# Conditioning products of the second network moved along VectorE's queue, and all their weight loads issued by GpSimd

## The reference, cut to what matters

```python
# first network, layer l
mod = (silu(c) @ w_ada[l] + b_ada[l]).reshape(b, 6, d)
sh_a, sc_a, gt_a, sh_f, sc_f, gt_f = [mod[:, i, None, :] for i in range(6)]
u = rms_norm(x, g_mix[l]) * (1 + sc_a) + sh_a          # ... three attention branches
x = x + gt_a * (merged @ w_out[l])
u = rms_norm(x, g_ffn[l]) * (1 + sc_f) + sh_f
x = x + gt_f * ((silu(u @ w_ffn_gate[l]) * (u @ w_ffn_up[l])) @ w_ffn_down[l])

# second network, layer i: the same with two vectors, for the tokens and for a context of 256 more
mod_lat = silu(c_2) @ ada_w_2[i] + ada_b_2[i]          # sh1, sc1, g1, sh2, sc2, g2
mod_ctx = silu(c_ctx_2) @ ada_w_2[i] + ada_b_2[i]
h = rmsnorm(x) * norm_g[i, 0] * (1 + sc1) + sh1        # i = 0: neighbourhood attention and spatial gating
x = x + g1 * rmsnorm(mixer(h), norm_g[i, 1])           # i = 1: retention, whose output is for the tokens alone
h = rmsnorm(x) * norm_g[i, 2] * (1 + sc2) + sh2
x = x + g2 * rmsnorm((silu(gate) * up) @ w_out, norm_g[i, 3])   # gate, up = dwconv3(h @ w_in)
```

## Time and profile before

| | us |
|---|---|
| median of 3 runs | 2406.58 (2398.55 to 2410.11) |
| the profiled execution | 2400.64 |
| its span | 2398.5 |
| PE busy | 2195.0 (92%) |
| DVE busy | 1633.2 (68%) |
| ACT busy | 1179.0 (49%) |
| POOL busy | 32.3 (1%) |

### The profile page before, as it was taken

One profiled execution on the slowest core, in us unless ns is written; L12 is line 12 of the kernel. 1 busy time (PEld: TensorE's weight loads), 2 busy tenths in 40 slices (PEclk: granted clock), 3 DMA queues, 4 the chain that ended last, 5 costly groups with the idle time before them and its releaser, 6 DMA issues.

```text
span 2398.5 us, 36407 instructions
## 1 busy us (share of the span) xinstructions
PE 2195.0 (92%) x13724; PEld 1925.3 (80%) x13724; DVE 1633.2 (68%) x2618; ACT 1179.0 (49%) x2032; POOL 32.3 (1%) x18
## 2 busy tenths in 40 slices
PE   1899999999999999999787979799998999898998
PEld 0797888999997889999674658578776888888998
DVE  5558876983658876973777688938484823565983
ACT  3355574653555655654534534435253323645763
POOL 4000000000000000000000000000000000000000
PEclk8899999999999999999898999899999999999999
DMA  6357734865557625864352145435351423214553
GB/s 264 132 177 237 230 112 158 270 216 176 165 190 236 215 97 177 294 206 158 117 182 88 54 157 176 158 105 201 107 176 61 141 93 118 97 55 139 187 184 114
DMA packets 107181, 385.08 MB, mean 161 GB/s; under 512 B 11664, under 2 KB 16272, under 8 KB 105744
## 3 DMA queue, kind: packets, MB, share of 16 engines
q1 hardware_dynamic: 75680, 272.66, 34.1%
q10 hardware_dynamic: 31344, 110.24, 13.3%
HBM read 381.81 MB, written 1.05 MB: 160 GB/s over the span
## 4 chain that ended last, share of the span: by engine, by line
PE 74%; DVE 13%; DMA 5%; ACT 5%; issue 2%; ACTq 1%; DVEq 0%; SPq 0%
PE ps L882 19%; PE ps L885 18%; PE ps L886 18%; DVE ada_junk L1935 5%; DMA work<-adas_in 4%; PE ps L899 3%; PE ps L902 3%; PE ps L903 3%; DVE ring_l L1910 2%; PE ps L1294 1%; DMA ring<-tape_in 1%; PE ps L915 1%; PE ps L918 1%; PE ps L919 1%; PE ps L1159 1%
## 5 line engine op out<-in xcount | busy, mean ns | idle before, releaser
L882 PE MATMUL ps<-part,ring_l 128*128 128x256 f32 (+1 forms) x3640 | 1123.6, 309 | 42.4 <-DVE part L1910 32.3
L885 PE MATMUL ps<-part,ring_r 128*128 128x256 f32 (+1 forms) x3640 | 1112.1, 306 | 0.0
L886 PE MATMUL ps<-part,ring_r 128*128 128x256 f32 (+1 forms) x3640 | 1110.9, 305 | 0.0
L1910 DVE TENSOR_TENSOR ring_l<-ring,ring_r 128x1024 fp32r<-128x1024 f32 x511 | 616.5, 1221 | 307.5 <-ACT ring_r L1341 304.9
L882 PEld LDWEIGHTS ps<-part,ring_l 128*128 128x128 f32 x3640 | 691.7, 190 | 95.8 <-DVE part L1910 38.9
L1341 ACT ACTIVATE ring_r<-ring 128x1024 fp32r<-128x1024 f32 x511 | 531.2, 1054 | 397.7 <-DMA ring<-tape_in 264.1
L885 PEld LDWEIGHTS ps<-part,ring_r 128*128 128x128 f32 x3640 | 690.2, 190 | 32.0 <-issue 1.2
L886 PEld LDWEIGHTS ps<-part,ring_r 128*128 128x128 f32 x3640 | 690.1, 190 | 30.8
L1935 DVE SCALAR_TENSOR_TENSOR ada_junk<-work 128x1024 bf16<-128x1024 f32 x272 | 345.7, 1271 | 39.2 <-DMA work<-adas_in 23.1
L899 PE MATMUL ps<-ring_l,part 128*128 128x512 f32 x264 | 106.3, 403 | 12.4 <-ACT work L1747 6.4
L902 PE MATMUL ps<-ring_r,part 128*128 128x512 f32 x264 | 105.9, 401 | 0.0
(11 more groups left out here) (226 smaller groups left out, 2052.5 us busy)
## 6 DMA issues: line engine op xcount, KB each, us to landing
ring<-tape_in SPq DMA_DIRECT2D x518, 512.0 KB, 3.3
work<-adas_in ACTq DMA_DIRECT2D x176, 512.0 KB, 4.3
work<-ada_first_in ACTq DMA_DIRECT2D x8, 1024.0 KB, 16.2
work<-bias_in ACTq DMA_DIRECT2D x1, 2048.0 KB, 7.9
work<-cond_in ACTq DMA_DIRECT2D x1, 1536.0 KB, 8.0
x<-x_t_in ACTq DMA_DIRECT2D x1, 1024.0 KB, 12.8
x<-ctx_in ACTq DMA_DIRECT2D x1, 1024.0 KB, 8.5
x<-dist_in ACTq DMA_DIRECT2D x1, 1024.0 KB, 8.5
```

The source lines that it names most:

```text
L882: mm = pe.matmul(dst, lhsT=wl, rhs=mr, start=(k == 0), stop=False)
L885: pe.matmul(dst, lhsT=wr, rhs=mr, start=False, stop=False)
L886: mm = pe.matmul(dst, lhsT=wr, rhs=ml, start=False, stop=(k == len(moving) - 1))
L1910: return dve.tensor_tensor(dst, whole, rounded_part.bitcast(F32), ALU.subtract)
```

## The change

Two things change, and no product is added or dropped.

First, all 176 loads are issued from POOL's queue, in two loops written at its end. POOL waits once for the first group of the first layer (`fox_f`), then, tile by tile, for the same semaphore for which ACT waited. ACT's queue no longer holds loads or their waits.

Second, DVE's products in the second network stand elsewhere. The 12 beside `na_qk` stay; none stand after the mixing products; 12 tiles stand beside `out0_0`; the other 56 stand in the wide feed-forward: one beside each of `conv0_0` to `conv0_15`, two beside each of `conv0_16` to `conv0_21`, and now also beside the output tiles (one beside each of `out1_0_f`, two beside `out1_1_0` to `out1_1_3`, one beside each of the twelve others). `modulation2` and `gain2` are called in smaller portions, each before its first reader.

```diff
-        ADA2_PAIRS = (6, 9)
-        ADA2_BEFORE = N_ADA - 2 * FT
-        def ada2_beside(f):
-            return range(ADA_LATE + ADA2_BEFORE + 2 * f, ADA_LATE + ADA2_BEFORE + 2 * f + 2)
+        ADA2_PAIRS = 6
+        ADA2_NORM = 3 * KD
+        ADA2_BESIDE, ada2_next = {}, ADA2_NORM
+        for c, (per_conv, per_out) in enumerate(((1, (1,) * KD), (1, (2,) * 4 + (1,) * 4), (2, (1,) * KD))):
+            for f in made_before(0, c):
+                ADA2_BESIDE[f"conv{f}"] = range(ada2_next, ada2_next + per_conv)
+                ada2_next += per_conv
+            for f in range(KD):
+                ADA2_BESIDE[f"out{c}_{f}"] = range(ada2_next, ada2_next + per_out[f])
+                ada2_next += per_out[f]
...
@@ gpsimd, after the first seven panels
+            pool.wait_ge(*done("fox_f", 0))
+            for l in range(DEPTH):
+                for t in range(N_ADA):
+                    if t >= ADA_SLOTS:
+                        pool.wait_ge(*ada_made(ada_last(t - ADA_SLOTS), l))
+                    elif l > 0:
+                        pool.wait_ge(*ada_made(ada_last(N_ADA - ADA_SLOTS + t), l - 1))
+                    pool.dma_start(ada_slot(t), adas[l * N_ADA + t]).then_inc(ada_landed[t % ADA_SLOTS], 16)
+            for t in range(ADA_LATE + N_ADA):
+                if t >= ADA_SLOTS:
+                    pool.wait_ge(*ada2_made(ada2_last(t - ADA_SLOTS)))
+                else:
+                    pool.wait_ge(*ada_made(ada_last(N_ADA - ADA_SLOTS + t), DEPTH - 1))
+                pool.dma_start(ada_slot(t), adas[DEPTH * N_ADA + t]).then_inc(ada_landed[t % ADA_SLOTS], 16)
@@ scalar, first network (and the same for load_ada2 and load_ada2_pair in the second)
-                def load_ada(t):
-                    if t >= ADA_SLOTS:
-                        act.wait_ge(*ada_made(ada_last(t - ADA_SLOTS), l))
-                    act.dma_start(ada_slot(t), adas[l * N_ADA + t])\
-                        .then_inc(ada_landed[t % ADA_SLOTS], 16)
...
@@ vector, second network
             ahead2("na_v3")
-            ada2_pairs(*ADA2_PAIRS)
...
-            for n in range(ADA2_PAIRS[1], ADA_LATE // 2):
+            for n in range(ADA2_PAIRS, ADA2_NORM // 2):
...
-            dve.wait_ge(*ada2_made(ada2_last(ADA_LATE - 1)))
-            modulation2(0, ADA_EARLY, N_ADA, 3)
+            dve.wait_ge(*ada2_made(ada2_last(ADA2_NORM - 1)))
+            modulation2(0, ADA_EARLY, ADA_EARLY + ADA2_NORM, 3)
...
             norm_in(2, 2, 3)
-            ada2_pairs(ADA_LATE // 2, (ADA_LATE + ADA2_BEFORE) // 2)
-            def beside(f):
-                for t in ada2_beside(f):
+            def beside(place):
+                if place == "out1_0":
+                    dve.wait_ge(*ada2_made(ada2_last(ADA_LATE - 1)))
+                    modulation2(0, ADA_EARLY + ADA2_NORM, N_ADA, 8)
+                    gain2(0, 3, 10)
+                for t in ADA2_BESIDE[place]:
                     ada2(t)
             feed_forward2(0, beside)
+            dve.wait_ge(*ada2_made(ada2_last(ADA_LATE + N_ADA - 1)))
+            modulation2(1, 0, ADA_EARLY, 0)
+            gain2(1, 0, 2)
             norm_out(1, 3)
             dve.wait_ge(*y2_scaled(2 * KD - 1))
-            dve.wait_ge(*ada2_made(ada2_last(ADA_LATE + N_ADA - 1)))
-            modulation2(1, 0, N_ADA, 0)
-            for n in range(4):
-                gain2(1, n, 2 + 2 * n)
             norm_in(3, 0, 0)
+            modulation2(1, ADA_EARLY, N_ADA, 3)
+            for n in range(1, 4):
+                gain2(1, n, 3 + 2 * n)
```

More of the change, by code:

```diff
@@ L2356, in feed_forward2 @@
                     rests(last)
+                    if c == 0:
+                        for f in range(KD):
+                            ahead2(f"out{1 + 2 * j}_{c}_{f}")
+                            beside(f"out{c}_{f}")
                     if c > 0:
```

50 lines of the change are left out of this document (12 added, 38 removed).

## The result

| | before | changed |
|---|---|---|
| median | 2405.41 us (4 runs) | 2375.18 us (2372.26 to 2382.55, 4 runs) |
| ratio | | 0.9881, interval 0.9848 to 0.9914 |
| ratio in a second series (5 rounds) | | 0.9918, interval 0.9890 to 0.9945 |
| span of the profiled execution | 2398.5 us | 2369.9 us |
| PE busy, mean granted clock | 2195.0, 0.962 | 2182.2, 0.968 |

The change is worth 0.8 to 1.2%, 20 to 29 us, by the ratios of the two series; forecast were 14.6, and 2388 us in a range of 2368 to 2420. The span of the profiled execution fell by 28.6 us. The terms of the sum did not all come out, as the stages show.

The account below looks back on a forecast made before the run. PE was taken to bound the kernel, busy 92% of the span. Terms 17.7 + 1.8 + 3.7 - 2.65 - 6.0 = 14.6 us gained, from 2400.6 to 2386.0, or 2392.0 by the median; forecast 2388, range 2368 to 2420.

Parts of the forecast that it names:

- First part of the wide feed-forward: At the start of `out1_0`: 20 fewer DVE products ahead end most of PE's wait and its slower clock; gain 17.7 us.
- Before the neighbourhood attention: Six loads leave ACT, so it copies the values earlier; gain 1.8 us, most of PE's 13.06 us gap stays.
- `out0_0`: Gating layer's output projection: 12 tiles instead of 14 bring `norm_out` earlier; gain 6.8 - 5d, 3.7 us.
- d: Time by which a load issued by POOL lands later than one issued by ACT; taken as 0.62 us from the cast.
- Beside `na_qk`: Twelve tiles there: ACT's late issues give back 0.45 us, later landings cost 5d; -2.65 us.
- First network: Attention, 64 tiles: eight waits without slack and steps with little slack, all charged to the span; -6.0 us.
- (A): Rival: POOL's loads land no later, d between 0 and 0.3; 19 to 27 us gained, 2374 to 2382; chance 0.22.
- the sign that the prediction named: Median from issue to landing of an ada tile, 4.3 us before: 4.9 by forecast, 4.3 to 4.6 by (A), over 5.7 by (B).
- (B): Rival: landing time decides in the 32 attention steps, 42 us per us beyond 1.34 us slack; slower, 2415 at 1.73; chance 0.14.
- (C): Rival: POOL writing load descriptors and DVE hold each other up, 88 loads at 0.62 us, 55 us, 2441; chance 0.08.
- (D): Rival: PE's wait at `out1_0` stays, from hidden tiles' rests and splits; gain there 3 to 10, 2394 to 2401; chance 0.11.
- closing tests of the prediction: Wrong if landing grows over 1.3 us and time still falls, or landing unchanged within 0.2 brings under 15 us.

Follow-up runs that it names:

- the block back: Changed kernel with two tiles again beside each of conv0_1 to conv0_8 and none beside out1_0_f; ratio to before 0.9952.
- second profile: The changed kernel profiled again, nothing altered, in a second series; ratio to before 0.9918.
- five memsets: Changed kernel with five small waited-for POOL memsets between wait and issue of each load, their target behind all other tiles; ratio to before 0.9977.
- the shifted one with five: Changed kernel with five POOL memsets before each load's issue and their 32-byte target ahead of the work area, moving it; ratio to before 1.0031.
- the shift alone: Changed kernel with 32 unused bytes of SBUF ahead of the work area, nothing else changed; ratio to before 0.9937.
- two memsets: Changed kernel with two small waited-for POOL memsets between wait and issue of each load, their target behind all other tiles; ratio to before 0.9913.
- the same shift and two memsets: Changed kernel with two POOL memsets before each load's issue and their 32-byte target ahead of the work area; ratio to before 0.9994.

## Why the prediction held, and where it did not

By the steps of the prediction, with the cuts of the table (profile of before against that of the changed kernel):

- **First part of the wide feed-forward**: forecast 17.7, measured 127.7 - 110.2 = 17.5. The reasoning held in both halves: PE stands for 2.43 us where 3.12 had been taken over from the next joint, and its clock no longer falls (1.00 against 0.62). The kernel with the block back shows the cause, and the one with ACT's loads at the new places has the same 110.2.
- **Before the neighbourhood attention**: forecast 1.8, measured 106.3 - 101.9 = 4.4 (2.9 in the second profile); PE's idle time in the stage fell by 3.0 in both, from 17.8 to 14.8. Mis-sized, and for a wrong reason. I took PE's L1216 at 1280.45 for the end of the values; they had been ready for copying earlier, as the kernel with POOL loads and old places shows, where ACT copies at 1277.16. What then decides is DVE: it was busy with products up to 0.34 us before ACT's part was ready, so they had to go too, which the term left out.
- **`out0_0`**: forecast 3.7, measured 73.4 - 70.3 = 3.1 (1.8 in the second profile). That the first two agree is luck. The term was 6.8 - 5d, so with ACT's loads, d = 0, it would be 6.8; the kernel with ACT's loads at the new places has the same 70.3. What the term had wrong is how early ACT and PE allow `norm_out`. The prediction took 4.5 us from PE's L1159 at 1405.73 to the end of ACT's root; in the rows themselves the root ends at 1413.51 + 0.63 = 1414.14, 8.4 us behind it, because PE's 16 products of the sums of squares take 7.03 us. That leaves 1417.38 - 1414.14 = 3.2 us to be won. Now DVE waits for that root, 0.51 us in the changed kernel and 2.40 with ACT's loads. In the second profile of the changed kernel it does not wait, so with POOL's landings DVE and the root are about even there.
- **Beside `na_qk`**: forecast -2.65, measured -1.2. With ACT's loads the stage took 67.5 and 66.4 us, with POOL's and the same products in it, without delay or shift, 67.0 to 69.0; so about -1 can be said.
- **First network**: forecast -6.0, measured -0.2 (353.4 to 353.6). This is the step that failed. d was about right where DVE feels it: 0.65 by the free slot, against 0.62 chosen, though 0.26 of it is the way to the issue, which the cast from which 0.62 was taken does not hold; that the two agree is partly luck. DVE's waits grew, by 2.9 us in the two stretches. The failed step is "DVE and PE are nearly even here, so I charge the whole of it to the span". The runs show about 2 us of PE's idle time in its place (13.6 with ACT's landings, 15.6 with POOL's), and stretches of the attention that are not longer (353.9 us with ACT's loads and 353.1 with POOL's, in the mean). Only with later landings does the charge become what the formula says: at five memsets the attention is 12.4 us longer than in the changed kernel's profile; at two it is 3.3 longer, which undelayed kernels reach too (356.8). Which instruction of the step gives DVE this slack was not measured.
- **Not in the sum**: 4.1 us in the tail (526.4 to 522.3) and 1.1 in the rest of the wide feed-forward. The prediction has no term for the tail, and the change touches no instruction in it; PE's pace differed there. In the changed kernel two thirds of the products of 256 columns in the thin feed-forward followed each other at 113.3 ns, in its second profile nearly all, and before all at 117.8. So this seems to belong to the kernel and not to the execution, but what in the kernel sets it is open.

Together 17.5 + 4.4 + 3.1 - 1.2 - 0.2 + 4.1 + 1.1 = 28.8, of 28.6 measured in the spans. Without the tail's pace the change is worth some 24 us in this profile. The ratios hold the tail too and can't part the two.

Of the rivals, (A), d between 0 and 0.3, has the time that came out, 2374 to 2382, and by the sign that the prediction named it would be taken for true: from issue to landing the median is 4.6, within the 4.3 to 4.6 of (A) and below the 4.9 of the forecast. But that sign leaves out the way to the issue; after a free slot the tile was 0.65 us later. With that in, it was the price that was low, not the delay. By the estimate from the Trainium skill, "DMA: Bandwidth & Descriptors", section "Latency and other measured facts" (0.4 us later), the time was to be 2382; the trace shows 0.3 us more from issue to landing over all loads (0.4 in the attention) and 0.26 us more before the issue. (B) is real as a mechanism: the kernel with five memsets, whose tiles land 1.3 us later than ACT's, lost 14 to 23 us against the changed one, and the shifted one with five lost 23 against the shift alone; POOL's own landings stay short of it. (C) has fallen: the mean of a product is 1270 ns with 176 loads on POOL, 1271 without, and DVE's splits take 1220 against 1221. This agrees with the Trainium skill, "SBUF — State Buffer", section "Who interferes with whom", which infers that a load's descriptors need the write side alone and that two-operand reads on DVE don't meet them. (D) fell with the block.

Neither of the two closing tests of the prediction arose: the landing grew by less than 1.3 us and by more than 0.2. It had no sign by which (A) and a low price could be told apart, and the time alone could not.

## What to carry to other kernels

Work that stands in a block on an engine with time to spare is worth spreading wherever the engine behind it is the bound: here 20 products fewer in front of one joint gave back 17.5 us, most of the gain, whoever issued the loads. Before charging a longer wait of a helper engine to the span, look how much the bound engine idles when it waits today: here 0.65 us more of each landing cost about 2 us of PE's idle time instead of 6, and the full price came only with landings 1.3 us later. When a blocked engine is freed, read what its successor will be waiting for next: here ACT and DVE were late by the same amount, and six loads taken off ACT alone gained nothing. And when a term comes out, check what now bounds the place: at `out0_0` it was the root, with no landing in it.

## What the runs showed of the hardware

- POOL issued a load 0.3 us after DVE was done with its slot, ACT within 0.05. The issue kept POOL for 0.53 us.
- The 114th load that POOL issued came late in all eleven profiles of kernels with 160 or 176 of them: 3.0 us in seven, 3.3 with two memsets ahead of each load, 3.8 with five. It moves with the count of loads and not with the time (it was at 1285, 1378 or 1526 us, among others) or with the number of POOL's instructions. What causes it was not measured.
- The pace of PE's products depends on where the operands lie, and not on that alone; the granted clock was 1.00 in the stretches of 30 and 40 us shown above. Taken over runs of 24 products, 512-column products of the wide feed-forward followed each other at 228.9 ns in nearly all runs of the kernels without the shift and at 233.3 in all of the three shifted ones; but in the kernel with ACT for the first network half of those behind the first part were at 233.3 too, at unshifted places. 256-column products of the tail followed at 117.8, or in part at 113.3 (mostly in the thin feed-forward of some kernels, the changed one in both of its profiles among them), and at 120.0 in the shifted ones. In the first network's stretches outside the attention they followed at 120.0, but with the shift alone mostly at 118.5 to 118.8; the kernel with the same shift and two memsets was mostly at 120.0. So the kernel with the shift alone was 11 us ahead of the changed one at `na_qk2` before it lost 21. A 32-byte tensor ahead of others is no neutral probe. What decides between two levels at the same addresses stays open.
